# Attention in a hybrid layer: raw queries with their norm as a factor on the scores

## The chip, the cores and the metric

One core of a Trainium2 chip (trn2) runs the whole layer as one program. The metric is device time in microseconds (us), as a median of several runs. The engines are TensorE (PE in the profile; its weight loads are PEld), VectorE (DVE), ScalarE (ACT), GpSimd (POOL) and SyncE (SP), which issues the loads.

## The reference, cut to what matters

One layer on x of 256 tokens by 2048, float32: a norm, a projection `h @ w_in` to queries, keys, values and the inputs of a second mixer (hgrn2), attention and hgrn2 side by side, an output projection, and a gated feed-forward block with a convolution. The change is in the attention, of 16 query heads of 64 channels on 2 key heads:

```
qc = rms_norm(q, q_gain)          # per token and head, over 64 channels
kc = rms_norm(k, k_gain)
scores = einsum(qc, band(kc)) * 64 ** -0.5      # 64 queries on 128 keys, two chunks of 64
scores = scores - slope[head] * |q_pos - k_pos|; invalid keys: -1e30
probs = softmax(concat([scores, sink[head]]))[..., :-1]
out = einsum(probs, band(v))
```

`rms_norm(q)` is `q / sqrt(mean(q * q) + eps) * gain`. The queries come out of a projection of x before its own norm r (one number per token), so q = r * q_raw.

## The kernel before, in words

Every large matmul is done as a split product: a weight unit (128 x 1024 floats, `raw`) is rounded to `w_hi` by ScalarE (`make_hi`, L448), and VectorE takes the rest `w_lo = raw - w_hi` (`make_lo`, L795). TensorE multiplies both with the high part of the input and `w_hi` with its low part. Four units make a quad, held in a ring of four. SyncE loads unit i of the next quad once `make_lo` has freed `raw`, `make_hi` waits for TensorE to have used `w_hi`, and TensorE waits for `units_split`. So TensorE's order of units is fixed by hand, and each unit of a quad is prepared while TensorE works on the three before it.

The projection runs with one quad for 256 columns. Quad 0 gives keys and values, quads 1 to 4 the queries, 4 heads each (4 groups, `Q_GROUPS`), quads 5 and 6 are the f and q inputs of the first pair of hgrn2 heads, and so on. A unit of quads 0 to 6 is 24 matmuls of 128x256 (L1334, L1336, L1337). The attention of group g is woven into quad g + 2, by a program of its own on each engine (`attention(g, quad)`):

- TensorE (L1480): unit 0; the mean over each head's channels of the squared queries, one fp32 matmul with `head_mean` (L1487), which leaves it in all rows of the head; unit 1; transposes of the last group's probabilities (`turn_p(g - 1)`); `scores(g)` in banks 2 and 3; `times_v(g - 2)` into bank 6; units 2 and 3.
- ScalarE (L565): squares (L568); Ln and Exp of the mean, 512 columns each (`att_rms`); `make_hi` 0 and 1; the copies of transposed P (`copy_pt`); exponentials of heads 0 and 1 (one Exp for each of the two token tiles, and a small one for the sink); `att_mix_hi`; `make_hi` 2; exponentials of heads 2 and 3; `make_hi` 3.
- VectorE (L970): the scaling of the last group's P by 1/denominator (`scale_p`, in pairs of heads; each head counts `p_scaled`); the scaling of the queries in QN by gain and norm (L978); `make_lo` 0; `bias_and_max` of heads 0 and 1 (L936: distance times slope plus scores; L942: maximum; L945: with the sink); `make_lo` 1; heads 2 and 3; `att_mix_lo`; `make_lo` 2; `take(quad)`, which reads the finished quad from its bank times the row of r; `make_lo` 3.

After group 3 come the q slot of the first hgrn2 pair (with the last `turn_p`, `copy_pt`, `times_v`), its i slot and its g slot, in which `head_scores` (L1533 to L1558) makes narrow matmuls in banks 2 to 5. GpSimd makes masks and constants at the start, and clears XK.

What orders the work is the semaphores. The lines that matter here:

```
pe.wait_ge(p_scaled, g * 4 + h + 1)      # turn_p, ahead of each head's transposes
pe.wait_ge(qk_normed, g + 2)             # scores
act.wait_ge(top_made, n + 1)             # exponentials of head n
dve.wait_ge(scores_made, g * 4 + 4)      # bias_and_max
```

## Time and profile before

| what | value |
|---|---|
| time, median of 3 runs | 1110.6 us (1110.41 to 1110.8) |
| the profiled execution's own time | 1110.93 us |
| its span, first to last instruction | 1109.2 us |
| TensorE busy | 1102.1 us (99%) |
| VectorE busy | 786.9 us (71%) |
| ScalarE busy | 589.4 us (53%) |
| GpSimd busy | 10.2 us (1%) |
| mean granted clock of TensorE | 1.000 (2.4 GHz) |
| attention stage, 37.2 to 111.0 us: VectorE busy in its five slots | 11.43, 12.27, 13.27, 12.94 and 12.54 us, of 13.6 to 15.5 |

The slots are those of quads 2 to 6. Matmuls are pipelined: one of 128x256 shows as 0.28 us long while the next starts 0.12 us after it. So TensorE's pace is read from the distance between starts, and a small wait can hide in the modelled length of a matmul. An fp32 matmul leaves two records, each a pass.

### The profile page before, as it was taken

Reading aid. Unit: us, or ns where it says so; the run is one execution under the profiler, and the core shown is the slowest. Engines: PE = TensorE matmul, PEld = TensorE weight load, DVE = VectorE, ACT = ScalarE, POOL = GpSimd, SP = SyncE. Lnnn points to the kernel's source line nnn. Section 1 sums busy time; section 2 is a strip of 40 time slices with the busy share of each in tenths; the row PEclk is TensorE's granted clock in tenths of the full one; section 3 lists DMA queues with packets and bytes.
Section 4 is the critical chain, followed back from the end, with each engine's and each line's share of the span. In section 5 each row is a group of like instructions: output and inputs, shape, how many; then the busy total and the mean of one; then the engine's idle time right before and its main releaser. Section 6 shows DMA issues by size and latency. Waiting matters only on the chain.

```text
span 1109.2 us, 18909 instructions
## 1 busy us (share of the span) xinstructions
PE 1102.1 (99%) x6705; PEld 957.7 (86%) x6705; DVE 786.9 (71%) x1168; ACT 589.4 (53%) x851; POOL 10.2 (1%) x40
## 2 busy tenths in 40 slices
PE   9999999999999999999999999999999999999998
PEld 8999888888888888888888888888888888888887
DVE  5888888889655587878778777877787644444443
ACT  7676566757545555555555555555555433333332
POOL 3000000000000000000000000000000000000000
PEclk9999999999999999999999999999999999999999
DMA  7544555564555555555555555555555555656562
GB/s 263 183 136 151 156 169 187 154 191 153 191 189 190 171 190 189 189 189 189 189 189 188 189 186 190 187 189 186 189 186 191 191 196 189 213 192 215 195 211 76
DMA packets 172514, 204.26 MB, mean 184 GB/s; under 512 B 6949, under 2 KB 140470, under 8 KB 172214
## 3 DMA queue, kind: packets, MB, share of 16 engines
q1 hardware_dynamic: 171302, 201.55, 56.6%
q10 hardware_dynamic: 1168, 2.11, 0.6%
q8 instruction: 28, 0.46, 0.2%
q14 instruction: 16, 0.13, 0.0%
HBM read 201.54 MB, written 2.10 MB: 184 GB/s over the span
## 4 chain that ended last, share of the span: by engine, by line
PE 99%; DVE 1%; ACT 0%; issue 0%; DVEq 0%; ACTq 0%
PE bank L1307 33%; PE bank L1315 17%; PE bank L1358 10%; PE bank L1357 10%; PE bank L1359 10%; PE bank L1512 3%; PE bank L1513 3%; PE bank L1514 3%; PE bank L1334 2%; PE bank L1336 2%; PE bank L1337 2%; PE bank L1273 1%; PE bank L1278 1%; PE bank L1551 0%; PE bank L1445 0%; PE bank L1487 0%
## 5 line engine op out<-in xcount | busy, mean ns | idle before, releaser
L795 DVE TENSOR_TENSOR w_lo<-raw,w_hi 128x1024 fp32r<-128x1024 f32 x379 | 461.9, 1222 | 258.3 <-ACT w_hi L448 257.7
L448 ACT CAST w_hi<-raw 128x1024 fp32r<-128x1024 f32 x379 | 397.2, 1051 | 415.8 <-PE bank L1359 177.5
L1307 PE MATMUL bank<-hs,w_hi 128*128 128x512 f32 x1600 | 383.4, 391 | 0.0
L1307 PEld LDWEIGHTS bank<-hs,w_hi 128*128 128x128 f32 x1600 | 293.8, 188 | 56.6
L1315 PEld LDWEIGHTS bank<-hs,w_lo 128*128 128x128 f32 x1600 | 205.5, 191 | 8.2 <-DVE hs L815 0.4
L1315 PE MATMUL bank<-hs,w_lo 128*128 128x256 f32 x1600 | 208.9, 283 | 0.2 <-DVE hs L815 0.2
L1357 PE MATMUL bank<-w_hi,gated 128*128 128x512 f32 x352 | 136.9, 389 | 0.0
L1358 PE MATMUL bank<-w_lo,gated 128*128 128x512 f32 x352 | 136.9, 389 | 0.0
L1359 PE MATMUL bank<-w_hi,gated 128*128 128x512 f32 x352 | 136.9, 389 | 0.0
L1357 PEld LDWEIGHTS bank<-w_hi,gated 128*128 128x128 f32 x352 | 66.1, 188 | 13.8
L1359 PEld LDWEIGHTS bank<-w_hi,gated 128*128 128x128 f32 x352 | 66.1, 188 | 13.7
L1358 PEld LDWEIGHTS bank<-w_lo,gated 128*128 128x128 f32 x352 | 66.1, 188 | 13.6
L1224 DVE SCALAR_TENSOR_TENSOR C<-U,cols,C 128x256 f32<-128x256 f32 x176 | 73.4, 479 | 0.0
L1334 PE MATMUL bank<-hs,w_hi 128*128 128x256 f32 x224 | 66.0, 295 | 0.2 <-DVE w_lo L795 0.2
L1337 PE MATMUL bank<-hs,w_lo 128*128 128x256 f32 x224 | 63.3, 283 | 0.0
L741 ACT ACTIVATE C<-U,cols 128x256 f32<-128x256 f32 x88 | 48.2, 595 | 28.4 <-DVE U L806 28.4
L1336 PE MATMUL bank<-hs,w_hi 128*128 128x256 f32 x224 | 63.3, 283 | 0.0
L1513 PE MATMUL bank<-w_lo,hs 128*128 128x512 f32 x128 | 49.9, 390 | 1.2 <-issue 1.2
L1512 PE MATMUL bank<-w_hi,hs 128*128 128x512 f32 x128 | 50.3, 393 | 0.0
L1357 PE MATMUL bank<-w_hi,mix 128*128 128x512 f32 x128 | 50.3, 393 | 0.0
L1359 PE MATMUL bank<-w_hi,mix 128*128 128x512 f32 x128 | 49.9, 390 | 0.0
L1514 PE MATMUL bank<-w_hi,hs 128*128 128x512 f32 x128 | 49.8, 389 | 0.0
(188 smaller groups left out, 901.5 us busy)
## 6 DMA issues: line engine op xcount, KB each, us to landing
raw<-in_w_ffn_up_dram SPq DMA_DIRECT2D x176, 512.0 KB, 3.4
raw<-in_w_ffn_down_dram SPq DMA_DIRECT2D x88, 512.0 KB, 3.6
raw<-in_w_in_dram SPq DMA_DIRECT2D x52, 512.0 KB, 3.6
raw<-in_w_in_dram SPq DMA_DIRECT2D x64, 256.0 KB, 2.9
raw<-in_w_out_dram SPq DMA_DIRECT2D x32, 512.0 KB, 3.8
xt<-in_x_dram SPq DMA_DIRECT2D x2, 1024.0 KB, 6.5
out_dram<-xt ACTq DMA_DIRECT2D x3, 512.0 KB, 6.3
out_dram<-xt ACTq DMA_DIRECT2D x2, 256.0 KB, 2.5
```

The costliest lines, as they stand in the source:

```text
L448: act.copy(w_hi[:, i, :], raw[:, i, :]).then_inc(units_hi, 1)
L795: dve.tensor_tensor(w_lo[:, i, :], raw[:, i, :], w_hi[:, i, :].bitcast(F32), ALU.subtract)\
L1307: m = pe.matmul(banks[b][:, :], w_hi[:, i, c], hs[:, 4 * i + k, :], start=(first and k == 0), stop=(final and k == 3))
L1315: m = pe.matmul(banks[b][:, 0:SEQ], w_lo[:, i, c], hs[:, 4 * i + k, 0:SEQ], start=(first and k == 0), stop=(final and k == 3))
L1334: pe.matmul(o, w_hi[:, i, c], x_hi, start=(tile == 0 and b == 0), stop=False, skip_group_check=True)
L1336: pe.matmul(o, w_hi[:, i, c], x_lo, start=False, stop=False, skip_group_check=True)
L1337: last = pe.matmul(o, w_lo[:, i, c], x_hi, start=False, stop=(tile == KT - 1), skip_group_check=True)
L1357: pe.matmul(banks[t][:, :], x_hi, hi, start=(k0 + k == 0), stop=False)
L1358: pe.matmul(banks[t][:, :], x_hi, lo, start=False, stop=False)
L1359: last = pe.matmul(banks[t][:, :], x_lo, hi, start=False, stop=(k0 + k == k_all - 1))
L1512: pe.matmul(o, x_hi, hi, start=(u == 0 and k == 0), stop=False)
L1513: pe.matmul(o, x_hi, lo, start=False, stop=False)
```

## The change

The queries are no longer normed before the scores. `take_q` copies them raw into QN; the gains of queries and keys and the factor 1/8 go into the keys (`qk_gain`). The norm is then a factor for each row of the scores: `q_scale`, one number for each token, pair and half, is (mean(q_raw^2) + q_eps)^-0.5, with q_eps = eps / r^2 by token.

- The mean is made by `mean_of_queries`: 16 matmuls with 32 tokens of SQ as the stationary operand and two columns of `head_mean` as the moving one, into 8 columns of bank 7. It stands behind `turn_p` in place of between units 0 and 1.
- ScalarE's Ln and Exp work on 4 and 8 columns and stand behind `make_hi` 1 in place of ahead of `make_hi` 0.
- `times_v(g - 2)` stands ahead of `scores(g)`. `scores` waits for the copy alone.
- VectorE's `bias_and_max` handles heads in pairs: for each head two fused instructions of 128x128 (score times `q_scale` plus penalty), then one maximum over both heads and one with the sink. ScalarE's exponentials wait for the pair.
- The penalties (distance times slope) of all heads are made by GpSimd: 12 at the start, ahead of clearing XK, 4 in the places of those used.
- The outputs of groups 2 and 3 go into banks 2 and 3, those of the scores, in place of bank 6; the wait for `att_lo` stands ahead of the first `head_scores` in place of the next f slot.
- The last `copy_pt` stands ahead of the FE instructions in the q slot in place of behind them and a `make_hi`.

```diff
+PENALTIES = 12
...
-        q_gain = sb("q_gain", [P, 1])
+        qk_gain = sb("qk_gain", [P, 1])
+        q_eps = sb("q_eps", [P, TT])
+        q_scale = sb("q_scale", [P, 2, TT, 2])
...
+        ahead_of_e = list(place)
         E = sb_at(place, "E", [P, NL + 1, 2, 2 * SEQ // 2])
+        penalty = sb_at(ahead_of_e, "penalty", [P, PENALTIES, KEYS])
...
-        bank_s, bank_p, bank_o_att, bank_m = bank[2:4], bank[4:6], bank[6], bank[7]
+        bank_s, bank_p, bank_m = bank[2:4], bank[4:6], bank[7]
+        banks_o_att = [bank[6], bank[6], bank[2], bank[3]]
+        head_means = bank_m[:, 0:8].rearrange("p (a t b) -> p a t b", a=2, t=TT)
...
-            for h in range(HEADS):
-                pool.memset(slopes[:, h:h + 1], 2.0 ** (-8.0 * (h + 1) / HEADS))
...
+
+            def make_penalty(n):
+                pool.tensor_scalar(penalty[:, n % PENALTIES, :], dist[:, :], 2.0 ** (-8.0 * (n + 1) / HEADS), None,
+                                   ALU.mult).then_inc(penalties_made, 1)
+
+            pool.wait_ge(dist_made, 4)
+            for n in range(PENALTIES):
+                make_penalty(n)
             pool.wait_ge(x_squared, 2 * TT)
             pool.memset(XK[:, :, :], 0.0).then_inc(xk_cleared, 1)
+            for n in range(PENALTIES, HEADS):
+                pool.wait_ge(biased, n - PENALTIES + 1)
+                make_penalty(n)
...
-            def att_rms(a, width):
-
...
+            def k_rms():
+
+                act.wait_ge(att_mean, 1)
+                act.activation(RS[:, 0:SEQ], bank_m[:, 0:SEQ], ACT.Ln, bias=eps[:, :]).then_inc(att_ln, 1)
+                act.wait_ge(att_ln, 1)
+                act.activation(RS[:, 0:SEQ], RS[:, 0:SEQ], ACT.Exp, scale=-0.5).then_inc(att_rs, 1)
+
+            def scale_of_queries(g):
+
+                if g:
+                    act.wait_ge(biased, g * 4)
+                act.wait_ge(att_mean, g + 2)
+                for t in range(TT):
+                    last = act.activation(q_scale[:, :, t, :], head_means[:, :, t, :], ACT.Ln, bias=q_eps[:, t:t + 1])
+                last.then_inc(att_ln, 1)
+                act.wait_ge(att_ln, g + 2)
+                act.activation(q_scale[:, :, :, :], q_scale[:, :, :, :], ACT.Exp, scale=-0.5).then_inc(att_rs, 1)
...
-            att_rms(0, SEQ)
+            k_rms()
...
-                act.wait_ge(top_made, n + 1)
+                act.wait_ge(top_made, n // 2 + 1)
...
-                act.copy(mix[:, 2 * g:2 * g + 2, 0:SEQ], bank_o_att[:, :].rearrange("p (a t) -> p a t", a=2))\
+                act.copy(mix[:, 2 * g:2 * g + 2, 0:SEQ], banks_o_att[g][:, :].rearrange("p (a t) -> p a t", a=2))\
...
@@ -567,9 +594,9 @@
                 act.wait_ge(w_in_taken, quad)
                 act.activation(SQ[:, :], QN[:, :, :].rearrange("p a t -> p (a t)"), ACT.Square)\
                     .then_inc(att_squared, 1)
-                att_rms(g + 1, 2 * SEQ)
                 make_hi(quad + 1, 0)
                 make_hi(quad + 1, 1)
+                scale_of_queries(g)
                 if g:
                     copy_pt(g - 1)
                 exponentials(g, 0)
@@ -616,6 +643,8 @@
                 sigmoid_exp(Q_F0 + 2 * j + 1, SG[:, :])
                 make_hi(quad + 1, 0)
...
+                if attention_ends:
+                    copy_pt(Q_GROUPS - 1)
...
                                    bias=lb[:, bass.ds(j * 2 + h, 1)]).then_inc(forget_scaled, 1)
                 make_hi(quad + 1, 1)
                 if attention_ends:
-                    copy_pt(Q_GROUPS - 1)
                     att_mix_hi(Q_GROUPS - 2)
...
+            def take_q(quad, src):
+
+                dve.wait_ge(units_used, (quad + 2) * RING)
+                dve.tensor_copy(QN[:, :, :], src[:, :].rearrange("p (a t) -> p a t", a=2)).then_inc(w_in_taken, 1)
+
             dve.memset(all_mean[:, :], 1.0 / HG_DIM).then_inc(all_mean_made, 1)
             for b in (2, 3):
...
-            dve.scalar_tensor_tensor(dist[first, P:KEYS], later, -1.0, later, ALU.mult, ALU.min)
-            dve.memset(dist[first, CHUNK:P], FAR)
+            dve.scalar_tensor_tensor(dist[first, P:KEYS], later, -1.0, later, ALU.mult, ALU.min)\
+                .then_inc(dist_made, 1)
+            dve.memset(dist[first, CHUNK:P], FAR).then_inc(dist_made, 1)
             make_lo(1, 0)
...
+            dve.tensor_reduce(ss[:, :], ss_part[:, :, 0:2], AX, ALU.add).then_inc(q_eps_from, 1)
+            dve.wait_ge(q_eps_from, 1)
+            dve.tensor_scalar(q_eps[:, :], ss[:, :], EPS / D_MODEL, EPS * EPS, ALU.mult, ALU.add).then_inc(x_summed, 1)
...
-            dve.tensor_scalar(q_gain[:, :], cols[:, Q_GAIN:Q_GAIN + 1], HEAD_DIM ** -0.5,
-                              None, ALU.mult)
+            dve.scalar_tensor_tensor(qk_gain[:, :], cols[:, Q_GAIN:Q_GAIN + 1], HEAD_DIM ** -0.5,
+                                     cols[:, K_GAIN:K_GAIN + 1], ALU.mult, ALU.mult)
+            dve.tensor_scalar(neg_sink[:, :], sink[:, :], -1.0, None, ALU.mult)
...
-            dve.scalar_tensor_tensor(QN[:, 0, :], FE[:, 0, :], cols[:, K_GAIN:K_GAIN + 1], RS[:, 0:SEQ],
-                                     ALU.mult, ALU.mult).then_inc(qk_normed, 1)
-            dve.wait_ge(qk_normed, 1)
+            dve.scalar_tensor_tensor(QN[:, 0, :], FE[:, 0, :], qk_gain[:, :], RS[:, 0:SEQ],
+                                     ALU.mult, ALU.mult).then_inc(k_normed, 1)
+            dve.wait_ge(k_normed, 1)
...
             for i in range(1, RING):
                 make_lo(2, i)
-            def bias_and_max(g, h):
-
-                n = g * 4 + h
+            def bias_and_max(g, pair):
+
+                first = g * 4 + 2 * pair
                 dve.wait_ge(scores_made, g * 4 + 4)
+                dve.wait_ge(att_rs, g + 2)
+                for half in range(2):
+                    h, n = 2 * pair + half, first + half
+                    if g:
+                        dve.wait_ge(p_transposed, n - 3)
+                    dve.wait_ge(penalties_made, n + 1)
+                    for t in range(TT):
+                        k = slice(t * P, (t + 1) * P)
+                        last = dve.scalar_tensor_tensor(PR[:, h, k],
+                                                        bank_s[half][:, pair * KEYS + t * P:pair * KEYS + (t + 1) * P],
+                                                        q_scale[:, pair, t, half:half + 1],
+                                                        penalty[:, n % PENALTIES, k], ALU.mult, ALU.add)
+                    last.then_inc(biased, 1)
+                dve.wait_ge(biased, first + 2)
                 if g:
-                    dve.wait_ge(p_transposed, n - 3)
-                dve.scalar_tensor_tensor(PR[:, h, :], dist[:, :], slopes[:, n:n + 1],
-                                         bank_s[h % 2][:, (h // 2) * KEYS:(h // 2 + 1) * KEYS],
-                                         ALU.mult, ALU.add).then_inc(biased, 1)
-                dve.wait_ge(biased, n + 1)
-                if g:
-                    dve.wait_ge(sink_made, n - 3)
-                dve.tensor_reduce(top[:, h, :], PR[:, h, :].rearrange("p (t k) -> p t k", t=TT), AX, ALU.max)\
-                    .then_inc(max_made, 1)
-                dve.wait_ge(max_made, n + 1)
-                dve.tensor_scalar(top[:, h, :], top[:, h, :], sink[:, n:n + 1], -1.0,
-                                  ALU.max, ALU.mult).then_inc(top_made, 1)
+                    dve.wait_ge(sink_made, first - 2)
+                tops = top[:, 2 * pair:2 * pair + 2, :]
+                dve.tensor_reduce(tops, PR[:, 2 * pair:2 * pair + 2, :].rearrange("p h (t k) -> p h t k", t=TT),
+                                  AX, ALU.max).then_inc(max_made, 1)
+                dve.wait_ge(max_made, g * 2 + pair + 1)
+                dve.scalar_tensor_tensor(tops, tops, -1.0,
+                                         neg_sink[:, first:first + 2].rearrange("p (h t) -> p h t", t=1)
+                                         .broadcast_to([P, 2, TT]), ALU.mult, ALU.min).then_inc(top_made, 1)
...
+                                  banks_o_att[g][:, :].rearrange("p (a t) -> p a t", a=2),
                                   mix[:, 2 * g:2 * g + 2, 0:SEQ].bitcast(F32), ALU.subtract)\
...
                     scale_p(g - 1, 0)
                     scale_p(g - 1, 1)
-                dve.wait_ge(att_rs, g + 2)
-                qn = QN[:, :, :].rearrange("p a t -> p (a t)")
-                dve.scalar_tensor_tensor(qn, qn, q_gain[:, :], RS[:, :], ALU.mult, ALU.mult)\
-                    .then_inc(qk_normed, 1)
                 make_lo(quad + 1, 0)
                 bias_and_max(g, 0)
+                make_lo(quad + 1, 1)
                 bias_and_max(g, 1)
-                make_lo(quad + 1, 1)
-                bias_and_max(g, 2)
-                bias_and_max(g, 3)
                 if g >= 2:
                     att_mix_lo(g - 2)
                 make_lo(quad + 1, 2)
-                take(quad, bank[quad % 2],
-                     QN[:, :, :] if g < Q_GROUPS - 1 else SG[:, :].rearrange("p (a t) -> p a t", a=2))
+                if g < Q_GROUPS - 1:
+                    take_q(quad, bank[quad % 2])
+                else:
+                    take(quad, bank[quad % 2], SG[:, :].rearrange("p (a t) -> p a t", a=2))
                 make_lo(quad + 1, 3)
...
                 kv = g // (Q_GROUPS // KV_HEADS)
-                pe.wait_ge(qk_normed, g + 2)
+                pe.wait_ge(w_in_taken, g + 2)
...
+            def mean_of_queries(g):
+
+                pe.wait_ge(att_squared, g + 2)
+                pe.wait_ge(att_ln, g + 1)
+                one_column_a_head = head_mean[:, :].rearrange("p (b d) -> p b d", b=2)[:, :, 0:1]
+                for pair in range(2):
+                    for t in range(TT):
+                        for s in NARROW_TILES:
+                            token = pair * SEQ + t * P + s.start
+                            last = pe.matmul(head_means[s, pair, t, :], SQ[:, token:token + NARROW],
+                                             one_column_a_head, start=True, stop=True)
+                last.then_inc(att_mean, 1)
+
...
                 pe.wait_ge(pt_made, 2 * g + 2)
-                if g:
-                    pe.wait_ge(att_lo, g)
+                if g == 1:
+                    pe.wait_ge(att_lo, 1)
+                if g >= 2:
+                    pe.wait_ge(biased, HEADS)
...
-                o = [bank_o_att[half * HEAD_DIM:(half + 1) * HEAD_DIM, :]
+                o = [banks_o_att[g][half * HEAD_DIM:(half + 1) * HEAD_DIM, :]
                      .rearrange("p (a t q) -> p a t q", a=2, t=TT) for half in range(2)]
...
                 unit_w_in(quad, 0, dst)
-                pe.wait_ge(att_squared, g + 2)
-                pe.matmul(bank_m[:, :], head_mean[:, :], SQ[:, :], start=True, stop=True)\
-                    .then_inc(att_mean, 1)
                 unit_w_in(quad, 1, dst)
                 if g:
                     turn_p(g - 1)
                 else:
                     pe.wait_ge(vt_made, 1)
-                scores(g)
+                mean_of_queries(g)
                 if g >= 2:
                     times_v(g - 2)
+                scores(g)
                 unit_w_in(quad, 2, dst)
                 unit_w_in(quad, 3, dst)
...
                 if j:
                     pe.wait_ge(hg_lo, j)
+                else:
+                    pe.wait_ge(att_lo, Q_GROUPS)
                 head_scores()
                 unit_i_and_g(quad, 3, j, RING + 3)
...
                 pe.wait_ge(w_in_taken, Q_F0 + 2 * j + 2)
-                if j == 0:
-                    pe.wait_ge(att_lo, Q_GROUPS)
                 for i in range(RING):
```

## Rows read from the trace of the kernel before

**Rows 1.** The page: span, and the chain that ended last by engine.
```profile
span 1109.2 us, 18909 instructions
...
PE 99%; DVE 1%; ACT 0%; issue 0%; DVEq 0%; ACTq 0%
```

**Rows 2.** TensorE in order of time around group 0's mean: start, us, instruction.
```profile
40.03 0.28 PE L1337 MATMUL bank<-hs,w_lo 128*128 128x256 f32 x1
40.15 1.02 PE L1487 MATMUL bank<-SQ,head_mean 128*128 128x512 f32 x2
...
41.13 0.28 PE L1336 MATMUL bank<-hs,w_hi 128*128 128x256 f32 x1
```

**Rows 3.** TensorE in order of time around the first `head_scores`.
```profile
129.90 0.39 PE L1514 MATMUL bank<-w_hi,hs 128*128 128x512 f32 x1
130.13 0.60 PE L1533 MATMUL bank<-E 128*128 128x128 f32 x4
130.66 0.45 PE L1540 MATMUL bank<-E,XK 128*64 128x64 f32 x8
130.94 1.51 PE L1551 MATMUL bank<-E,XK 128*64 128x32 f32 x110
...
132.32 0.45 PE L1558 MATMUL bank<-QB,KB 128*32 128x32 f32 x30
132.70 0.50 PE L1512 MATMUL bank<-w_hi,hs 128*128 128x512 f32 x1
133.03 0.40 PE L1513 MATMUL bank<-w_lo,hs 128*128 128x512 f32 x1
```

**Rows 4.** TensorE in order of time, group 2, and the next transposes of P.
```profile
71.91 1.04 PE L1273 MATMUL bank<-ident,PR 128*128 128x128 f32 x8
72.88 1.10 PE L1445 MATMUL bank<-kz,QN 64*64 64x128 f32 x32
73.91 0.65 PE L1472 MATMUL bank<-PT,vt 128*64 128x256 f32 x4
...
74.93 0.38 PE L1334 MATMUL bank<-hs,w_hi 128*128 128x256 f32 x1
...
87.39 1.04 PE L1273 MATMUL bank<-ident,PR 128*128 128x128 f32 x8
```

**Rows 5.** VectorE in order of time, then two of its lines.
```profile
74.08 0.48 DVE L936 SCALAR_TENSOR_TENSOR PR<-dist,slopes,bank 128x256 f32<-128x256 f32 x1 [1.28 <-PE bank L1445]
...
76.28 1.22 DVE L795 TENSOR_TENSOR w_lo<-raw,w_hi 128x1024 fp32r<-128x1024 f32 x1
...
82.11 1.23 DVE L795 TENSOR_TENSOR w_lo<-raw,w_hi 128x1024 fp32r<-128x1024 f32 x1
...
84.74 0.76 DVE L960 TENSOR_TENSOR PR<-PR,den 128x256 f32<-128x256 f32 x2
...
132.68 0.46 DVE L1119 COPY ST<-bank 64x64 f32<-64x64 f32 x2 [2.09 <-PE bank L1558]
...
L1162 DVE SCALAR_TENSOR_TENSOR OG<-bank,o_ss,GE x16: 340/343/352, 144.9 to 292.7; 128x128 f32<-128x128 f32 x16
...
L802 DVE TENSOR_REDUCE U<-bank x44: 681/684/684, 392.8 to 868.5; 128x256 f32<-128x512 f32 x44
```

**Rows 6.** ScalarE in order of time, group 2.
```profile
75.31 0.40 ACT L544 ACTIVATE PR<-PR,top 128x128 f32<-128x128 f32 x1 [1.12 <-DVE top L945]
...
78.16 1.05 ACT L448 CAST w_hi<-raw 128x1024 fp32r<-128x1024 f32 x1 [0.21 <-PE bank L1337]
...
81.04 1.05 ACT L448 CAST w_hi<-raw 128x1024 fp32r<-128x1024 f32 x1
```

**Rows 7.** GpSimd, VectorE and TensorE in order of time at the start.
```profile
5.27 0.88 POOL L414 TENSOR_SCALAR_AFFINE_SELECT block_mask<-block_mask 128x256 f32<-128x256 f32 x1
...
28.98 1.23 DVE L795 TENSOR_TENSOR w_lo<-raw,w_hi 128x1024 fp32r<-128x1024 f32 x1
...
30.58 0.47 PE L1334 MATMUL bank<-hs,w_hi 128*128 128x256 f32 x1
```

More of the change, by code:

```diff
@@ L117, in hybrid_layer @@
         all_mean = sb("all_mean", [P, P])
-        slopes = sb("slopes", [P, HEADS])
+        neg_sink = sb("neg_sink", [P, HEADS])
         sink = sb("sink", [P, HEADS])
@@ L246, in hybrid_layer @@
             sem("x_transposed"), sem("h_hi"), sem("h_lo"), sem("u_summed"))
-        att_squared, att_mean, att_ln, att_rs, qk_normed = (
-            sem("att_squared"), sem("att_mean"), sem("att_ln"), sem("att_rs"), sem("qk_normed"))
+        att_squared, att_mean, att_ln, att_rs, k_normed = (
+            sem("att_squared"), sem("att_mean"), sem("att_ln"), sem("att_rs"), sem("k_normed"))
         kz_made, v_transposed, vt_made = (
@@ L518, in _ @@
             spread_row(0)
-            def att_rms(a, width):
-                act.wait_ge(att_mean, a + 1)
-                act.activation(RS[:, 0:width], bank[7][:, 0:width], ACT.Ln, bias=eps[:, :])\
-                    .then_inc(att_ln, 1)
-                act.wait_ge(att_ln, a + 1)
-                act.activation(RS[:, 0:width], RS[:, 0:width], ACT.Exp, scale=-0.5).then_inc(att_rs, 1)
+            def k_rms():
[12 more added lines that the diff above has]
+                act.activation(q_scale[:, :, :, :], q_scale[:, :, :, :], ACT.Exp, scale=-0.5).then_inc(att_rs, 1)
             act.wait_ge(w_in_taken, 1)
@@ L925, in _ @@
             dve.wait_ge(kz_made, 4)
[L926 removed]
+            take_q(1, bank[1])
             for i in range(1, RING):
                 make_lo(2, i)
[L930 to L932 removed]
+            def bias_and_max(g, pair):
+                first = g * 4 + 2 * pair
                 dve.wait_ge(scores_made, g * 4 + 4)
[L934 to L946 removed]
```

4 lines of the change are left out of this document (1 added, 3 removed).

## The prediction

> **What bounds the kernel now.** I read the page first: its chain of waits is 99% TensorE, in a span of 1109.2 us [rows 1]. A busy TensorE need not be a dense one, so I went to its instructions in order of time. What the reader is to see there is the start-to-start distance. In the w_in units it is 0.12 us for every 128x256 matmul, and it is kept right up to each small job of attention and resumed right behind it [rows 2, 4]. No matmul of the attention stage waits for VectorE, ScalarE or a load. So a change pays here only by what it takes off TensorE's own stream, and it loses only by a wait that reaches TensorE. VectorE and ScalarE are not the bound, but they feed it over a chain with little room, so I read them last, in order of time [rows 5, 6].
>
> **The mean of the queries.** Before, each group runs one fp32 matmul of 128x512. The weight unit's last matmul starts at 40.03, and the second one behind the mean at 41.13 [rows 2]. That is 1.10 us for what is two steps of 0.12 without it, so the mean costs 0.86 us, four times 3.44 us in all. In its place come 16 fp32 matmuls of 32 stationary columns and 2 moving ones, spread over four column strips. An fp32 matmul leaves two records (x2 in [rows 2]), so these are 32 records. The nearest rows are the narrow tiles of `head_scores`, same stationary width and same strips [rows 3]: 30 records of L1558 take 132.32 to 132.70, 12.7 ns each, and 110 records, nearly all of 16 moving columns, take 130.94 to 132.32, 12.5 ns each. Halving the moving columns saved nothing, so I take 32 x 12.6 = 0.40 us for 2 columns as well.
>
> A change of tile shape costs something too: the first wide matmul behind the narrow ones is followed after 0.33 us (132.70 to 133.03), where 0.23 is the rhythm (129.90 to 130.13) [rows 3]. The new matmuls stand between transposes (full tile) and `times_v` or `scores` (half tiles), where a change was before as well, so one change is added, 0.05 to 0.10 us. I take 0.48 us a group: 4 x (0.86 - 0.48) = 1.5 us saved. Bounds: below, 0.40 us and no change of shape, 1.8 us saved. Above, the L1540 records (64 wide, two strips): eight in 0.28 us, 35 ns each [rows 3], which for 32 makes 1.12 us, and with a change of shape 1.22: 4 x 0.36 = 1.4 us lost. I stay by the near end, since the width and the strips are those of L1558 and not those of L1540.
>
> The Trainium skill speaks against this part: TensorEngine Tiling, section Instruction Overhead, says that a matmul has some 60 cycles of overhead however few columns it moves. By that, as an estimate, 32 passes at 25 ns make 0.80 us and the saving would be nearly nothing. The trace disagrees where four strips are in use: 12.6 ns a record.
>
> `scores`, `turn_p` and `times_v` issue the same instructions, only `times_v` now stands ahead of `scores`. The banks of the last two outputs move the wait for `att_lo` from the next f slot to `head_scores` at 130.13 [rows 3], two weight quads behind the last unit of attention. Nothing for both.
>
> **VectorE and ScalarE: cheaper, but later.** Leaving out the norm of QN, Ln and Exp over 512 columns, saves them some 2 us a group that TensorE never waited for: worth nothing by itself. What matters is the chain from scores to the scaled probabilities, because `turn_p` stands in TensorE's queue with everything behind it. Take group 2, with 0 at its `turn_p` (71.91); the next `turn_p` is at 87.39, 15.48 later [rows 4].
>
> TensorE after: transposes 0.97, means 0.45, `times_v` 1.02, scores 1.04, then four units of 2.88: next `turn_p` at 15.0. Before, the scores start at 0.97 and VectorE's first score instruction at 74.08, so 1.20 behind them. After, the scores start at 2.44 and VectorE at 3.64, 1.47 us later. That is the price of the new order, and it hits groups 2 and 3 alone; in groups 0 and 1 it is 0.45.
>
> The pair of heads took VectorE 2.20 us (74.08 to 76.28), and ScalarE could start on the first head after 1.23 (75.31) [rows 5, 6]. After, a pair is four fused instructions of 128x128, one reduce over 512 and one tiny one. A fused one reading a bank is 0.34 us (L1162), overlapped by its neighbour to some 0.26; a reduce over 512 is 0.68 (L802) [rows 5]. So 1.13 + 0.04 + 0.68 + 0.04 + 0.18 = 2.07: slightly less for VectorE, but ScalarE's first exponential starts only then, at 5.7 instead of 3.4. Of these 2.3 us ScalarE's idle 0.21 ahead of make_hi takes back a little (78.16) [rows 6], so its last `make_hi` comes 2.1 us later, at 81.04 + 2.1, and VectorE's last `make_lo` starts at 12.3 instead of 10.2 (82.11). The four scaled heads then come at 14.3, 14.6, 15.4 and 15.7 (before: the last at 84.74 + 0.76, 13.6). TensorE wants them at 15.0, 15.24, 15.48 and 15.73. So the room of 1.9 us is used up, but not overdrawn, beyond some 0.05 us. Groups 0 and 1 start a microsecond earlier against a deadline of 14.0 and keep 0.3 to 0.4 us. I put 0.1 us for all of it. With that cover gone, each further 0.1 us of lateness costs 0.1 us in each of groups 2 and 3.
>
> Behind the last group, `copy_pt(3)` moves ahead of the FE instructions, and its two copies (about 1 us) with the lateness of `scale_p` make the forget chain some 2.5 us late. Its units have room of 0.6 us and more by the same arithmetic, and VectorE idles 2.09 us ahead of L1119 [rows 5]; the lateness ends there. Nothing, with up to 0.5 us in the range.
>
> **The start.** GpSimd makes 12 penalties of 128x256 once `dist` is made, some 20 us ahead of the first scores. The nearest row is an affine_select of that size, 0.88 us [rows 7], so at most 10.6 us: ready in time. The last four are asked for by group 0 and used by group 3. `q_eps` adds one instruction of a few columns ahead of `x_summed`; the weight unit that ScalarE converts at that time hides it. A price that no row shows is what GpSimd does to VectorE: they work at the same time now, and the `make_lo` that ends at 30.21 has 0.37 us before TensorE takes it at 30.58 [rows 7]. Slowed by nothing, it costs nothing; doubled (1.23 more), it costs 0.9 us. I take nothing, since the trace has no sign of either.
>
> **Sum.** -1.5 + 0.1 = -1.4 us. The profiled execution took 1110.93 us, 0.3 above the median of 1110.6; its span is 1109.2. After: a span of 1107.8, and a median of 1109.2 us, 0.13% less.
>
> **Rivals.** (a) My forecast: a little saved, and within the 0.2% (2.2 us) that a measurement of this kernel can tell from no change. By the bounds of the mean (1.8 us) and a room that is overdrawn by some 0.2 us in each group (0.7 us saved), it lies at 1108.7 to 1109.9.
> (b) Faster by over 0.2%. That needs a mean under 0.3 us a group: at 0.20 us, 4 x 0.66 = 2.6 us, 1108.0. For: 2 columns are an eighth of the narrowest measured. Against: 16 and 32 columns run at one pace.
> (c) An instruction has a floor that four strips don't hide when it moves next to nothing. Half way to L1540's 35 ns, at 24 ns a record, a mean takes 0.77 + 0.1 and nothing is saved, 1110.6; at 35 ns it is the 1.4 us lost, 1112.0 [rows 3]. For: nothing here has run so few columns. Against: 12.6 ns. GpSimd slowing the start ends in the same place: 0.9 us, 1110.1. The rule of the Trainium skill above (TensorEngine Tiling, Instruction Overhead) is this rival's, and by its 25 ns, an estimate, it comes out at the first of these times.
> (d) Slower: `turn_p` waits in each group. The place is `p_scaled` in turn_p, the price 1.0 us a group and as much in the forget chain if the chain of pairs is 1.3 us longer than I worked out (heads in pairs wait for both): 5 x 1.0 - 1.5 = 3.5, 1114.1. With five such places it turns the sign from 0.3 us each on, and passes 0.2% from 0.75 each on. For: the room falls from 1.9 to about zero. Against: each term has a row, and a slack of 0.3 in half the groups.
>
> **Chances.** (a) 0.58, (b) 0.12, (c) 0.20, of which nearly all is within 0.2%, (d) 0.10, of which 0.09 beyond it. So faster 0.12, same 0.79, slower 0.09. The range goes from (b)'s time to the bound of (c): 1108.0 to 1112.0.
>
> **What would show it.** In the profile after: an inserted piece of TensorE of 0.4 to 0.5 us between transposes and `times_v`, and 14.0 us (groups 0, 1) and 15.0 us (groups 2, 3) from one `turn_p` to the next. ScalarE's first exponential 2.1 us behind VectorE's first score instruction. No gap of over 0.1 us ahead of the transposes of P. GpSimd done before the first scores, and VectorE's `make_lo` still at 1.22 us beside it. Wrong if a record of the new means takes over 20 ns, or if transposes of P have VectorE as what they waited for.

## The result, and the profile after

The changed kernel takes 1113.2 us (median of 12 runs; the kernel before 1110.6 in the same job): a ratio of 1.0021, 95% interval 1.0013 to 1.003. One of the 12 executions took 3888.56 us, which no trace explains, and the ratio leaves it out. The changed kernel is slower by 0.2%. The forecast was 1109.2, and 1113.2 lies outside its range. The profiled execution of after took 1113.92 us, with a span of 1112.2 against 1109.2 of before, so 3.0 us are to be found.

First the parts that the prediction worked out. The kernel after, TensorE in order of time around the small means of groups 0, 1 and 3, with the transposes of group 2's slot:

```profile
42.50 0.28 PE L1380 MATMUL bank<-hs,w_lo 128*128 128x256 f32 x1
42.71 0.43 PE L1504 MATMUL bank<-head_mean,SQ 128*32 128x2 f32 x32
43.07 1.10 PE L1488 MATMUL bank<-kz,QN 64*64 64x128 f32 x32
...
55.73 1.34 PE L1316 MATMUL bank<-ident,PR 128*128 128x128 f32 x8
56.99 0.43 PE L1504 MATMUL bank<-head_mean,SQ 128*32 128x2 f32 x32
...
70.01 1.03 PE L1316 MATMUL bank<-ident,PR 128*128 128x128 f32 x8
...
85.00 1.04 PE L1316 MATMUL bank<-ident,PR 128*128 128x128 f32 x8
85.97 0.43 PE L1504 MATMUL bank<-head_mean,SQ 128*32 128x2 f32 x32
86.33 0.65 PE L1530 MATMUL bank<-PT,vt 128*64 128x256 f32 x4
```

A mean takes 0.36 us from its first start to the next line's (42.71 to 43.07, 85.97 to 86.33), where the 128x512 matmul of [rows 2] cost 0.86. From one `turn_p` to the next it is 15.0 us (70.01 to 85.00), as forecast. The eight transposes of the first `turn_p` take 1.26 us (55.73 to 56.99) instead of 0.97: 0.3 us of waiting inside them, and 14.3 us to the next `turn_p` instead of the 14.0 forecast. VectorE and ScalarE of group 2, which answer to [rows 5, 6]:

```profile
73.56 1.13 DVE L979 SCALAR_TENSOR_TENSOR PR<-bank,q_scale,penalty 128x128 f32<-128x128 f32 x4 [2.31 <-PE bank L1488]
74.72 0.69 DVE L988 TENSOR_REDUCE top<-PR 128x4 f32<-128x512 f32 x1
...
75.64 0.40 ACT L571 ACTIVATE PR<-PR,top 128x128 f32<-128x128 f32 x1 [2.47 <-DVE top L991]
```

The first exponential starts 2.08 us behind VectorE's first score instruction. So attention went as worked out, and the first `head_scores`, at 130.13 before [rows 3], starts at 128.12: 2.0 us gained. What took 5 us from there on? The waits of TensorE say it in one row of each kernel. Before, then after:

```profile
PE bank L1513 <- issue: 1.2, 1, 1.2
```

```profile
PE bank L1614 <- issue: 3.7, 1, 3.7
```

"issue" is time in which the engine waited for nothing that the profile shows. No semaphore and no load ends these 3.7 us. TensorE in order of time there, in `head_scores` of pair 3, the last pair (the pairs count from 0):

```profile
274.00 0.60 PE L1589 MATMUL bank<-E 128*128 128x128 f32 x4
...
276.20 0.43 PE L1614 MATMUL bank<-QB,KB 128*32 128x32 f32 x28
280.32 0.27 PE L1614 MATMUL bank<-QB,KB 128*32 128x32 f32 x2 [3.69 <-issue]
280.52 0.80 PE L1568 MATMUL bank<-w_hi,hs 128*128 128x512 f32 x1
281.11 0.63 PE L1569 MATMUL bank<-w_lo,hs 128*128 128x512 f32 x1
281.54 0.63 PE L1570 MATMUL bank<-w_hi,hs 128*128 128x512 f32 x1
...
285.74 0.40 PE L1400 MATMUL bank<-w_hi,mix 128*128 128x512 f32 x1
285.97 0.40 PE L1401 MATMUL bank<-w_lo,mix 128*128 128x512 f32 x1
```

The same place before (L1357 is the first matmul of the next section, as L1400 is in after), and ahead of it the 1.2 us of before, in the wide units behind `head_scores` of pair 2:

```profile
231.31 0.39 PE L1512 MATMUL bank<-w_hi,hs 128*128 128x512 f32 x1
232.88 0.39 PE L1513 MATMUL bank<-w_lo,hs 128*128 128x512 f32 x1 [1.18 <-issue]
...
277.13 0.60 PE L1533 MATMUL bank<-E 128*128 128x128 f32 x4
...
279.33 0.67 PE L1558 MATMUL bank<-QB,KB 128*32 128x32 f32 x30
279.93 0.50 PE L1512 MATMUL bank<-w_hi,hs 128*128 128x512 f32 x1
...
282.79 0.39 PE L1357 MATMUL bank<-w_hi,mix 128*128 128x512 f32 x1
```

In after, two records of thirty are held back for 3.7 us, in the middle of a run of equal ones. Behind them the wide matmuls come every 0.43 us instead of every 0.23. The table by stretches of the kernel after shows the clock beside it (behind the times: busy us and count of PE, PEld, DVE, ACT, POOL, then the granted clock, the DMA share, GB/s):

```profile
274.00:276.00 2.00, 2.00 (x105) 1.83 (x105) 2.00 (x2) 1.05 (x1) 0.00 (x0) 1.00 0.31 89
276.00:278.00 2.00, 0.63 (x72) 0.52 (x61) 1.38 (x6) 0.00 (x0) 0.00 (x0) 1.00 0.88 266
278.00:280.00 2.00, 0.00 (x0) 0.00 (x0) 1.59 (x4) 0.00 (x0) 0.00 (x0) 0.70 0.78 260
...
282.00:284.00 2.00, 2.00 (x6) 1.62 (x5) 1.09 (x4) 0.00 (x0) 0.00 (x0) 0.50 0.73 244
...
286.00:288.00 2.00, 2.00 (x10) 1.65 (x9) 0.93 (x1) 2.00 (x4) 0.00 (x0) 1.00 0.00 0
```

TensorE's granted clock fell from 2.4 to 1.2 GHz at 278.8, while the engine stood still, and came back at 285.6. From the start of `head_scores` to the next section's first matmul it is 11.74 us after (274.00 to 285.74) and 5.66 before: 6.1 us lost, 3.7 by the stall and 2.4 by the clock and the last records behind it. By 274.00 after was ahead by 3.1 us (2.0 of the attention stage and the start, and 1.1 of pair 2, whose "issue" wait of before is gone). 6.1 - 3.1 = 3.0 us, the whole difference of the spans.

So two questions: what holds instructions back where nothing is waited for, and why did the change move it from pair 2 to pair 3 and make it three times as long?

### The profile page after: what moved, and what is told of

It is laid out like the page before. It is cut to its first block, busy times and chain, and to the rows that moved or that the text cites. A ratio compares the mean times of both kernels' runs of the same rounds, so it can differ in the third digit from the quotient of the medians.

```text
span 1112.2 us, 19161 instructions
## 1 busy us (share of the span) xinstructions
PE 1102.5 (99%) x6825; PEld 959.0 (86%) x6825; DVE 783.6 (70%) x1166; ACT 585.2 (53%) x855; POOL 27.2 (2%) x40
## 4 chain that ended last, share of the span: by engine, by line
PE 98%; DVE 1%; DMA 1%; issue 0%; ACT 0%; SPq 0%; DVEq 0%; ACTq 0%
PE bank L1350 33%; PE bank L1358 17%; PE bank L1401 10%; PE bank L1402 10%; PE bank L1400 10%; PE bank L1568 3%; PE bank L1569 3%; PE bank L1570 3%; PE bank L1377 2%; PE bank L1379 2%; PE bank L1380 2%; PE bank L1316 1%; DMA xt<-in_x_dram 1%; PE bank L1607 0%; PE bank L1488 0%
## 5 line engine op out<-in xcount | busy, mean ns | idle before, releaser
L1400 PE MATMUL bank<-w_hi,gated 128*128 128x512 f32 x352 | 136.9, 389 | 0.0
L1400 PEld LDWEIGHTS bank<-w_hi,gated 128*128 128x128 f32 x352 | 66.1, 188 | 13.8
L1400 PE MATMUL bank<-w_hi,mix 128*128 128x512 f32 x128 | 50.3, 393 | 0.0
```

The source lines that it names most:

```text
L1400: pe.matmul(banks[t][:, :], x_hi, hi, start=(k0 + k == 0), stop=False)
```

## The theory, and its rivals

Section 3 of the profile's page, the DMA queues, has one that carries instructions (packets, MB, share). Before and after:

```profile
q8 instruction: 28, 0.46, 0.2%
```

```profile
q8 instruction: 29, 0.48, 0.2%
```

That is about 16 KB a packet. TensorE's stream, with what is looped counted once, is 7383 instructions before and 7628 after (a matmul record is two instructions, weights and product). At 256 instructions a packet that is 28.8 and 29.8 packets, and the queue shows 28 and 29. I laid blocks of 256 over the records. With one origin, the stalls of both kernels, pair 2's before and pair 3's after, stand at the first instruction of a block. The change adds 245 instructions ahead of the pairs, 240 of them the four small means (64 instructions each for 4). 245 is 256 - 11, so each edge of a block moved by 11 instructions against the code. `head_scores` is 312 instructions in 2.8 us, where a wide unit spends 2.8 us on 24. A block that begins early in it is used up in some 1.3 us (275.20 to 276.45 in pair 3 of after). Counted in instructions into `head_scores`, the edges for pairs 0 to 3 (29 apart, since a pair has 797) lie at 129, 100, 71, 42 before, and at 140, 111, 82, 53 after.

Theory A: the place of the edges decides, whatever the instructions are. Theory B: `head_scores` of pair 3 collides with the weight loads, at times that the change has shifted. Theory C: the rearranged waits of the change do it, the prediction's rival (d) at another place.

## The experiments

**1 to 4: move the edges without the change, and with it.** `keep_busy(n)` is n products of 128 x 128 at the start of the kernel, a warm-up, and `fill(n)` is n products of 32 x 2 columns. Nobody reads their results. Each product of either is 4 instructions.

```
e1, of before:   keep_busy(10) -> keep_busy(7)
e2, of after:    keep_busy(10) -> keep_busy(13)
e3, of after:    keep_busy(10) -> keep_busy(5); fill(50)
e4, of before:   keep_busy(10) -> keep_busy(5); fill(47)
```

e1. 

> The kernel before with 7 in place of 10 warm-up matmuls at its start, 12 instructions less in TensorE's queue; nothing else. Theory A (instruction blocks): TensorE gets its instructions in blocks of 256, one ahead, and stalls where a block is used up sooner than the next one arrives; head_scores, 312 instructions in 2.8 us, does that if a block's edge lies 30 to 85 instructions into it. With 12 less, the edges lie in head_scores where the changed kernel has them, 82 and 53 instructions in for the pairs 2 and 3. So the stall of 1.4 us of pair 2 shrinks to 0.2, and pair 3 stalls by some 3.7 us, with 2.4 us of half clock behind it: 1110.6 - 1.2 + 5.9 = 1115.3, between 1112 and 1116. Theory B (weight loads): the stall of the changed kernel comes from a collision with loads whose times the attention has shifted; 12 instructions change nothing: 1110.6. Theory C (my rival d, waits of the transposes of P): 1110.6 too.

Measured: 1114.6 us, ratio 1.0029 (1.0017 to 1.0041). The kernel before, with three warm-up products less, has the loss of the change and more:

```profile
277.88 0.43 PE L1558 MATMUL bank<-QB,KB 128*32 128x32 f32 x29
281.81 0.22 PE L1558 MATMUL bank<-QB,KB 128*32 128x32 f32 x1 [3.50 <-issue]
```

B and C fall as they stand, since nothing of the change is in this kernel.

e2. 

> The changed kernel with 13 in place of 10 warm-up matmuls, 12 instructions more; the edges lie where the kernel before has them (127, 98, 69 and 40 instructions into head_scores). Theory A: stalls of about 1.4 us in pair 2 and 0.2 in pair 3 in place of 6.1 us with the clock's part: 1113.2 - 6.1 + 1.5 = 1108.6, between 1108.0 and 1109.5. Theory B: 1113.2. Theory C: 1113.2.

Measured: 1109.5 us, ratio 0.9988 (0.9979 to 0.9997), no wait in pair 3, and the 1.2 us of pair 2 in before are back. A is right, and 0.9 us too hopeful by the size.

e3. 

> The changed kernel with 5 warm-up matmuls and 50 tiny ones (32 by 2) in place of 10, 180 instructions more; edges 215, 186, 157 and 128 instructions into head_scores, so that the block that reaches past it is never used up quickly. Theory A: no gap over 0.3 us in any head_scores, clock 1.000: 1113.2 - 6.1 = 1107.1, between 1106.5 and 1107.8. Theory B and C: 1113.2.

e4. 

> The kernel before with 168 instructions more in the same way; edges 216, 187, 158 and 129 instructions into head_scores. Theory A: it loses its stall of pair 2 (1.4 us) and the 0.2 us of pair 3: 1109.0, between 1108.6 and 1109.5; so that with both kernels free of stalls the change itself is worth 1.9 us. Theory B: 1110.6.

Measured: e3 1108.7, ratio 0.9981 (0.9972 to 0.999); e4 1110.3, ratio 0.9994 (0.9985 to 1.0003). Neither has an "issue" wait in `head_scores`, but the padding itself delayed the start (first `head_scores` at 129.68 in e3 for 128.12 in after, at 130.89 in e4 for 130.13 in before), so both are over a microsecond above what was expected and outside the bounds given. Against each other they are the change free of edges: 1108.7 - 1110.3 = -1.6 us by the medians, -1.2 by the profiled spans (1107.3 and 1108.5). The prediction had -1.4. The starts differ, though: the first w_in matmul comes at 12.98 in e3 and at 12.51 in e4. Counted from there, e3 is ahead by 1.6 us in the profiles too.

**5: shift the edges by a real edit.** The small means of groups 0 and 1 with weight tiles 64 wide, 64 instructions fewer.

```
-                        for s in NARROW_TILES:
+                        for s in COLUMN_TILES if g < 2 else NARROW_TILES:
```

> The kernel after, with the small means of query groups 0 and 1 made by weight tiles 64 tokens wide instead of 32: 8 calls a group instead of 16, so 64 instructions fewer in TensorE's stream ahead of the pairs; the start and everything else is as in the kernel after. Theory A (instructions come in blocks of 256, and a block whose edge falls some 30 to 85 instructions into head_scores ends before the next is there): the edges move from 140, 111, 82, 53 to 204, 175, 146, 117 instructions into head_scores of pairs 0 to 3; no stall and no half clock there, span 1105.9, time 1107.3 (bounds 1106.5 to 1108.3). Theory B (head_scores of pair 3 collides with weight loads, wherever the blocks lie) and theory C (the new waits of the change itself set the loss): as after, 1113.2. A 64-wide tile may cost a little more or less than two of 32: within 0.2 us over both groups.

Measured: 1107.75, ratio 0.9973 (0.9963 to 0.9984), span 1106.0, no "issue" wait of TensorE. It beats both kernels. Its 64-wide mean, though:

```profile
42.58 0.63 PE L1504 MATMUL bank<-head_mean,SQ 128*64 128x2 f32 x16
43.14 1.10 PE L1488 MATMUL bank<-kz,QN 64*64 64x128 f32 x32
```

16 records in 0.56 us, 35 ns each, against 11 ns of 32-wide ones. That is 0.2 us a group dearer, 0.4 in all: the expectation's "within 0.2 us over both" missed.

This gives a check on all kernels whose blocks cause no wait. From the first `head_scores` to the end of the span e3, e4, e5 and the later e7, e12 and f2 take 977.6 to 977.7 us, whether the change is in them or not. Before takes 979.1 and after 984.0. So all that tells after from before behind 128 us is the edges.

**6: the same 12 instructions elsewhere.** 

> The kernel after with 12 more instructions in TensorE's stream, as in the earlier run with 12 more, but put beside the small means of query group 3 instead of into the warm-up at the start: three tiny matrix products (32 x 2 columns) whose result nobody reads. Theory A: only the count ahead of the pairs matters, not the place: edges 128, 99, 70, 41, time 1109.5 (1109.0 to 1110.3) as with 12 at the start. A rival of it (the longer warm-up at the start gave the gain, by the clock or the loads' order): as after, 1113.2.

Measured: 1109.3, ratio 0.9988 (0.9979 to 0.9997), the same as e2, with a wait of 1.1 us in pair 2. Only the count ahead of the pairs matters. That was the last rival by which a longer warm-up could have been the gain.

**7: the price of the small means alone.** 

> The kernel after with one 128x512 mean a query group in the place of the small means (so the scale of the queries is computed from wrong numbers; the work of every engine is otherwise the same), and the same short warm-up and tiny products ahead as the run with 180 more instructions, sized so that the edges fall at the same 216, 187, 158, 129. No stall expected in head_scores. It stands against that run (1108.73): the difference is the price of the small means alone. By the prediction's term (0.86 against 0.48 us a group) 1.5 us more, 1110.2; by the rows of the kernel after (0.86 against 0.36) 2.0 us more, 1110.7; if small means are worth nothing, 1108.7 and the order of the attention's work carries the gain.

Measured: 1110.5, ratio 0.9998 (0.9989 to 1.0007). Against e3's 1108.7 the small means are worth 1.8 us, between the two sizes expected. All of the change's gain is here. By the medians the rest of it costs 0.2 us (e7 against e4), but e7 starts 0.4 us later (its first w_in matmul at 12.87), and from there to the end the two profiles agree within 0.1 us. So the rest of the change, without its edges, is worth nothing that shows.

**8: make the block last longer instead.** Wide unit 3 is issued inside `head_scores`, ahead of level 1.

```
                 for l in reversed(range(NL - 1)):
+                    if l == 1:
+                        unit_between()        # unit_i_and_g(quad, 3, j, RING + 3)
```

> The kernel after with the same instructions in the same number, but weight unit 3 of each pair's quad issued between the levels of head_scores (after 120 of its 312 instructions) instead of behind it, so a block of instructions lasts 2.8 us longer there. Theory A: the stall of 3.7 us in pair 3 shrinks by about those 2.8 us to 0.9 us, and the half clock behind it mostly goes: 4 to 5 us less in pair 3, 1108.7 (bounds 1107.5 to 1110.5; the last levels are ready 2.8 us later, which VectorE may feel). Theory B and C: 1113.

Measured: 1117.2, ratio 1.0062 (1.0048 to 1.0076). The stall did what A says, the time did not. TensorE's waits:

```profile
PE bank L1639 <- DVE ST L1178: 3.5, 3, 1.4
PE bank L1400 <- DVE ST L1178: 1.9, 1, 1.9
...
PE bank L1616 <- issue: 0.8, 1, 0.8
```

3.7 us of stall became 0.8, and in the profiled execution, at 1115.9, the clock stayed at 2.4 GHz. In three of the five executions it did not: 1117.2 to 1118.7 at a mean of 0.997 or 0.998, so the median is one of those. The last levels are ready 2.8 us later, VectorE's chain to ST starts later, and TensorE waits for it at every `output`: 5.4 us in all. The room there was under 2.8 us, which I had named and priced too low. Of the 8.3 us that the profiled execution takes over 977.7 behind the first `head_scores`, these waits are 6.2; the other 2 stay open.

**9 to 11: the edge in small steps** (4 or 8 instructions added at the last means, 8 taken from the warm-up).

> The kernel after with 4 more instructions ahead of the pairs (one tiny matrix product beside the small means of group 3): edges 136, 107, 78, 49 instructions into head_scores. So far, stall against edge: 53 or 54: 3.7 us; 70 or 71: 1.2 to 1.6; 82 or 83: 0 to 0.5; 41 or 42: none; 99 and above: none. Theory A1 (the block that begins at the edge is simply used up too soon; the line through those points falls by 0.13 us an instruction): pair 2 at 78: 0.5 us; pair 3 at 49: 4.2 us and half clock, 1114. Theory A2 (the next block is asked for by a part of the engine that runs some 50 instructions ahead of the array; an edge within those of the start of head_scores has been asked for while the wide unit before it still ran): pair 2 0.5 us, pair 3 none, time 1108.0.

> The same with 8 more instructions: edges 132, 103, 74, 45. Both theories: pair 2 at 74 about 1.0 us. A1: pair 3 at 45 4.7 us and half clock, 1115. A2: pair 3 none, 1108.5.

> The same with 8 fewer instructions (two products less in the warm-up at the start): edges 148, 119, 90, 61. Both theories: pair 2 at 90 nothing, pair 3 at 61 a stall of 2.6 us. What it tells: whether half clock follows this shorter stall too (1112.0) or not (1109.7), as it did not after the stalls of 1.6 us and below.

Measured: e9 1108.7 (ratio 0.9981, 0.9971 to 0.9991), e10 1108.7 (0.9982, 0.9972 to 0.9992), e11 1112.3 (1.0008, 0.9998 to 1.0018). With the other kernels this gives the table below. Times are us of the trace; "head_scores" is its start, "edge run" the time at which TensorE reaches the edge, "packet" the start of the q8 packet next to it, and "wait" the "issue" wait at the next edge, 256 instructions on.

```
edge   kernel, pair    head_scores  edge run  packet   wait
 41    e2, 3           275.44       276.46    275.39   none
 45    e10, 3          274.57       275.65    274.86   none
 49    e9, 3           274.11       275.25    274.87   0.5
 53    after, 3        274.00       275.20    277.94   3.7
 54    e1, 3           275.68       276.89    279.31   3.5
 61    e11, 3          273.77       275.14    277.99   3.2
 70    e2, 2           225.38       226.80    228.80   1.2
 71    before, 2       227.23       228.66    230.44   1.2
 74    e10, 2          225.40       226.85    228.21   0.3
 78    e9, 2           225.42       226.88    228.37   none
 82 and over: none
```

From 53 on the wait shrinks with the edge, as A1 has it: a later edge leaves wide matmuls in the block, which last longer. Below 53 it falls from 3.7 to 0.5 within 4 instructions, as A2 has it: where the packet is under way before the edge is reached, little or nothing is lost. In all seven rows with a wait TensorE goes on 2.2 to 2.5 us behind the start of the packet, so the wait is what is left of these 2.4 us when the block before is used up. Pair 3 of e9 starts only 0.1 us later than that of after (274.11 and 274.00), so its gain of 3.2 us is not one of another time against the loads. In e11 the clock fell to 1.2 GHz as well, at 280.8, behind a wait of 3.2:

```profile
PE bank L1570 <- issue: 3.2, 1, 3.2
```

Its executions part in two: three at 1109.8 to 1110.8 with a mean clock of 1.000, five at 1112.3 to 1113.6 with 0.997 or 0.998. So the clock's part is about 2 us. After had the lower clock in 10 executions, and 1.000 in one, at 1110.88.

**12: the outputs' banks.** Of e5, only this part undone:

```
-        banks_o_att = [bank[6], bank[6], bank[2], bank[3]]
+        banks_o_att = [bank[6], bank[6], bank[6], bank[6]]
```

with `pe.wait_ge(att_lo, g)` in `times_v` for every g but 0. 

> The version with the 64-wide small means in groups 0 and 1 (1107.75), with one part of the change undone: the attention outputs of all four groups go to bank 6 again, and each waits until VectorE has taken the one before. Same number of instructions, same edges (204, 175, 146, 117). If the other banks are worth something, times_v of group 3 now waits for VectorE's part of group 2's output: from the order of the work (one wide unit, 2.8 us, between the two on TensorE; exponentials and copies of ScalarE and VectorE in between) some 1 to 4 us at one place, 1108.7 to 1111.5. If they are worth nothing: 1107.7.

Measured: 1110.0, ratio 0.9991 (0.9982 to 1.0), 2.3 us over e5. Some 0.6 us of it is a later start (the first w_in matmul at 11.94, for 11.37 in e5), the rest the wait. It is where it was expected, behind the third output:

```profile
107.45 0.65 PE L1528 MATMUL bank<-PT,vt 128*64 128x256 f32 x4 [1.80 <-DVE mix L1012]
```

With the order that the change gives ScalarE (`copy_pt(3)` first), the two banks are needed. The kernel before, with one bank and its own order, has no such wait, so the two banks gain nothing over it.

**13 and 14: why the fetch is late.** In the table above the packet jumps from 274.87 to 277.94. In after the weight loads leave the DMA engines idle from 274.0 to 275.0, and then they fill them (0.88 from 276 to 278 in the table by stretches).

```
f1, of after: w_out quads c = 0 and 1 load 16 of 512 columns
f3, of e2:    the forget weights of pairs 1 to 3 load 16 of 512 columns
```

> The kernel after, where the first two quads of each output group's weights are loaded only in 16 of 512 columns (the rest of the tile keeps old weights, so the output is not the layer's); TensorE's instructions and the edges (140, 111, 82, 53) are the same. Theory D (the fetch of the next block queues behind the weight loads' packets): beside pair 3 the DMA engines are nearly idle, the fetch packet comes within 1 us of the edge instead of 2.7, and the stall falls from 3.7 to under 1 us, without half clock; span 1107.5 or less. Theory E (a fetch takes its 5 us by itself, whatever else moves): stall 3.7 us as before, fetch packet again 2.7 us behind the edge, span 1112.

> The kernel after with 12 more warm-up instructions (edges 128, 99, 70, 41, stall of 1.2 us in pair 2), with the weights of the next pair's forget gates loaded only in 16 of 512 columns (so they are wrong); these loads run beside head_scores. Theory D: pair 2's stall goes, 1108.2. Theory E: it stays at 1.2 us, 1109.5. If other loads (the second half of the i and g weights) are those beside head_scores, D shows less of a change; the DMA row beside the burst will tell.

Measured: f1 1109.2, ratio 0.9986 (0.9977 to 0.9996); f3 1108.6, ratio 0.9983 (0.9974 to 0.9993). In f1 the DMA share is 0.20 where it was 0.88, the packet comes 1.1 us behind the edge (275.00, 276.07) and not 2.7, and the wait is 2.0 us (the stretch, then the wait):

```profile
276.00:278.00 2.00, 0.43 (x49) 0.32 (x39) 1.30 (x6) 0.00 (x0) 0.00 (x0) 1.00 0.20 25
```

```profile
PE bank L1623 <- issue: 2.0, 1, 2.0
```

In f3 pair 2's packet comes 0.4 us behind the edge and not 2.0, and its wait is gone. So both theories hold for a part, and D's "under 1 us, without half clock" missed: 1.7 of the 3.7 us go with the loads' traffic, and 2.0 stay without it. The profiled execution of f1 is the one of its ten with a lower clock (1111.2 us); the others, at 1.000, took 1108.8 to 1109.5. From the packet's start to the first instruction of the block it is 2.4 us in both (277.94 to 280.32, 276.07 to 278.44).

**15: the edges moved at no price.** Warm-up products of 512 columns, 2 instead of 10 of 128: 32 instructions fewer. 

> The kernel after with the 10 warm-up products of 128 columns ahead of the first transposes made into 2 of 512 columns: 32 instructions fewer, nothing else changed. Theory A: edges 172, 143, 114, 85, no stall beyond 0.3 us in head_scores, the 32-wide means kept everywhere, so 0.4 us under the version with 64-wide means (1107.75): 1107.3 (1106.9 to 1108.0). The warm-up is 256 columns shorter, about 0.4 us, and TensorE waits for the first loads behind it anyway. If the start suffers (clock or order), it shows ahead of the first w_in unit, by up to 1 us.

Measured: 1107.7, ratio 0.9975 (0.9966 to 0.9985), span 1105.9, no "issue" wait in `head_scores`. It equals e5, and not the 1107.3 expected. The 0.4 us of the narrower means are there, and the first `turn_p` gives them back: its transposes take 1.56 us, where those of e5 take 1.15. TensorE came earlier to probabilities that were not ready earlier. The waits of f2 (that for `xt`, at the start, is 0.5 in e5):

```profile
PE bank L1316 <- DMA xt<-in_x_dram: 0.8, 1, 0.8
...
PE bank L1316 <- DVE PR L1007: 0.3, 1, 0.3
```

## Why the prediction was wrong

**The step that failed** is the sum, "-1.5 + 0.1 = -1.4 us", and the rule that it was built by: a change "loses only by a wait that reaches TensorE", where the waits looked for were those for VectorE, ScalarE and loads. The means entered as "32 records" at 0.48 us a group. The prediction counted what each instruction takes and what it waits for, and gave their number no term at all. 32 records and their weight loads in the place of two cost 0.36 us where they stand. In four groups they are 240 of the 245 instructions that moved the edges of the blocks, and this cost 6.1 us in pair 3, some 200 us later, and gave back the 1.1 us of pair 2. No rival had it. I had [rows 1] with "issue 0%" before me and took it as nothing. The waits of before had the row of 1.2 us in L1513, shown above, which is this same mechanism, and asking what ended that wait would have led to it.

**What was right.** The means: 0.48 us a group forecast, 0.36 measured, 1.5 us saved forecast, 1.8 by e7 against e3. The record of a 32-wide tile is 11 ns, so 2 columns in the place of 16 did not slow it: rival (c) falls. The estimate of 25 ns a pass, from the Trainium skill, TensorEngine Tiling (Array Packing), section Instruction Overhead, does not hold with four strips (11 ns); with two strips e5 has 35. The chain: 2.08 us and 15.0 us came as worked out. Its slack was nearly enough: nothing is lost in groups 2 and 3, and 0.3 us inside the first `turn_p`, for group 0, where I had 0.3 to 0.4 us of room. That room was not there, and f2 names VectorE's scaled P as what is waited for, one of the signs of being wrong. Rival (d), at 1.0 us in five places, falls. The sum for the change by itself was -1.4. From the first w_in matmul to the first `head_scores` before takes 118.2 us and after 116.6, which says -1.6, as e3 against e4 does: four means at 0.5 us less, and some 0.3 lost in `turn_p`. That it comes so close is in part luck, a mean priced 0.1 us a group too dear against a wait that was not expected.

**What was off without harm.** GpSimd. The prediction bounded 12 penalties by 10.6 us from a row of 0.88 each:

```profile
21.97 14.98 POOL L441 TENSOR_SCALAR penalty<-dist 128x256 f32<-128x256 f32 x12 [13.18 <-DVE dist L919]
```

It took 15.0, 1.25 us each, and ended at 36.95, still ahead of the first scores at 43.07. VectorE's `make_lo` beside it kept a median of 1.22 us. Also 0.4 us of the start of after (29.93 against 30.33 for the same matmul) are not the change's: the second load of x landed at 8.35 us in the profiled execution of after and at 8.74 in that of before.

**The blocks of 256.** The Trainium skill, Runtime: NRT & Kernel Launch, section Instruction fetch mechanics, states that an engine takes its instructions in blocks of 16 KiB, 256 instructions, and fetches the next while it runs the present one. The traces here agree (about 16 KB a packet, stalls at one place in 256). It also says that crossing an edge is "mostly hidden". In this kernel it is at all edges but one or two, and there it costs up to 3.7 us, and 2 more by the clock.

**What stays open.** Why the packet of an edge at 53 comes 3 us later than that of one at 49. Traffic explains 1.7 us of it (f1). It could be that TensorE's sequencer asks for a block from some way ahead of the array, and so early only where the instructions ahead are long. That fits the rows: among wide matmuls the packet is seen 2 to 5 us ahead of its edge (304.2 and 309.1 in after). But no run shows the asking itself, and the jump between 49 and 53 is more than the traffic. Why the clock fell in some executions of after, e1, e8, e11 and f1 and not in others was not tried.

## What to carry to other kernels

Count the instructions of a change as well as their time. Where an engine runs hundreds of short ones in a few microseconds, the edge of a block of 256 that falls early into them can cost more than the edit saves, and any edit ahead of it moves that edge. An "issue" wait of over a microsecond in the middle of equal records is its sign. Before judging an edit by under 0.5% of the time, shift the stream by some tens of instructions and measure again: here 12 harmless instructions moved either kernel by about 4 us.

## What the hardware showed that I had not expected

- The same kernel before takes 1110.6 or 1114.6 us, by three warm-up products more or less.
- A TensorE that stood still for 3.7 us came back at 1.2 GHz and stayed there until 285.6, at 0.43 us a wide matmul for 0.23. Behind a wait of 2.0 us (f1) the clock was lower in one execution of ten, and behind one of 1.2 us (e2) in none of eleven.
- fp32 products of 2 moving columns: 11 ns a record in four strips of 32, 35 ns in two of 64.
- A fetched block is usable 2.2 to 2.5 us after its packet starts, though the packet itself takes 1.0.
- Beside idle DMA engines (share 0.20, f1) the fetch packet of an edge started 1.1 us behind it, beside weight loads (0.88, after) 2.7.
- GpSimd's tensor_scalar of 128x256 took 1.25 us beside a busy VectorE in the start, 0.84 us a piece later (two in 1.67 us, at 45.72).
